# Input projection of a hybrid trunk step: 26 of 28 pairs of weight tiles by seven half-size block products in place of eight

## What is computed

```
h = rms_norm(x, g_norm) * (1 + scale) + shift          # scale, shift, gate from silu(c) @ w_ada
proj = h @ w_in                                         # 1024 -> 7168
u   = proj[glu_value] * sigmoid(proj[glu_gate])
y   = silu(layer_norm(depthwise_conv31(u)))
y_a = (y * silu(proj[conv_z])) @ w_a_out
p   = windowed_mean(proj[pool_in]) - proj[pool_in]      # windows 2, 4, 8, 16 by group
y_b = (group_matmul(p) * scale * silu(proj[pool_z])) @ w_b_out
m   = sigmoid(proj[merge_a]) * y_a + sigmoid(proj[merge_b]) * y_b
out = rms_norm(x + gate * (m @ w_out), g_final)         # and the new states of both branches
```

## Time and profile before

| | us |
|---|---|
| median of 3 runs | 993.92 (993.38 to 994.63) |
| profiled execution, its own time | 993.59 |
| span of the profiled execution | 991.8 |
| TensorE busy in the span | 977.4 |
| VectorE busy | 664.6 |
| ScalarE busy | 245.4 |
| mean granted clock of TensorE | 0.997 of full speed |

### The profile page before, as it was taken

How to read it: one execution, slowest core, us unless ns; L and a number is a source line. 1 busy time by engine, 2 the same in 40 slices (tenths; PEclk the granted TensorE clock), 3 DMA queues, 4 the chain that set the end, 5 groups by cost and what they waited for, 6 DMA issues and landing times.

```text
span 991.8 us, 14051 instructions
## 1 busy us (share of the span) xinstructions
PE 977.4 (99%) x6256; PEld 960.1 (97%) x6256; DVE 664.6 (67%) x666; ACT 245.4 (25%) x263; POOL 1.9 (0%) x12
## 2 busy tenths in 40 slices
PE   8999999999999999999999999999999999999997
PEld 5699999999999999999999999999999998999996
DVE  1868985727897663888764689969878743342346
ACT  5331122221212221112212111123623512122242
POOL 0000000000000000000000000000000000000000
PEclk9999999999999999999999999999999999999998
DMA  9612221231230231122024122113961173124104
GB/s 373 251 44 64 88 78 55 86 122 43 67 116 27 97 123 48 59 86 97 28 76 142 43 76 100 55 54 129 368 250 43 36 306 128 43 88 190 43 1 171
DMA packets 32252, 106.46 MB, mean 107 GB/s; under 512 B 7616, under 2 KB 14144, under 8 KB 28736
## 3 DMA queue, kind: packets, MB, share of 16 engines
q1 hardware_dynamic: 28016, 92.75, 26.7%
q10 hardware_dynamic: 4176, 12.82, 3.4%
HBM read 82.76 MB, written 22.79 MB: 106 GB/s over the span
## 4 chain that ended last, share of the span: by engine, by line
PE 96%; DMA 1%; DVE 1%; ACT 0%; issue 0%; SPq 0%; DVEq 0%
PE ps L490 31%; PE ps L493 31%; PE ps L491 31%; DMA bf<-x_t 1%; PE aux L420 1%; DVE bf L948 1%; PE aux L426 0%; PE aux L472 0%; DVE hf L1202 0%; PE ps L420 0%; PE aux L663 0%; PE ps L433 0%; PE aux L655 0%; PE ps L467 0%; ACT L755 0%
## 5 line engine op out<-in xcount | busy, mean ns | idle before, releaser
L491 PE MATMUL ps<-hr,w_hi 128*128 128x344 f32 x1536 | 486.8, 320 | 0.0
L490 PE MATMUL ps<-hr,w_hi 128*128 128x344 f32 x1344 | 426.5, 320 | 0.6 <-DVE hr L957 0.6
L981 DVE SCALAR_TENSOR_TENSOR conv_y<-conv_u,par_all,conv_y 128x1024 f32<-128x1024 f32 x240 | 308.1, 1284 | 22.6 <-PE ps L493 16.0
L491 PEld LDWEIGHTS ps<-hr,w_hi 128*128 128x128 f32 x1536 | 289.2, 188 | 0.0
L493 PE MATMUL ps<-hr,w_lo 128*128 128x344 f32 x1344 | 285.1, 320 | 0.0
L490 PEld LDWEIGHTS ps<-hr,w_hi 128*128 128x128 f32 x1344 | 253.1, 188 | 2.4 <-issue 1.6
L493 PEld LDWEIGHTS ps<-hr,w_lo 128*128 128x128 f32 x1344 | 224.9, 188 | 0.0
L906 DVE TENSOR_TENSOR w_lo<-w_raw,w_hi 128x1024 fp32r<-128x1024 f32 (+1 forms) x86 | 98.8, 1149 | 83.7 <-ACT w_hi L706 80.8
L706 ACT ACTIVATE w_hi<-w_raw 128x1024 fp32r<-128x1024 f32 (+1 forms) x86 | 85.5, 995 | 280.2 <-PE ps L493 269.4
L490 PE MATMUL ps<-gr,w_hi 128*128 128x344 f32 x384 | 123.3, 324 | 0.0
L491 PE MATMUL ps<-gr,w_hi 128*128 128x344 f32 x384 | 121.8, 320 | 0.0
(11 more groups left out here) (129 smaller groups left out, 564.8 us busy)
## 6 DMA issues: line engine op xcount, KB each, us to landing
w_raw<-w_main SPq DMA_DIRECT2D x78, 512.0 KB, 3.6
ada_raw<-w_ada SPq DMA_DIRECT2D x8, 1024.0 KB, 20.2
bf<-x_t SPq DMA_DIRECT2D x4, 1032.0 KB, 8.6
sig_a<-stage_lo ACTq DMA_DIRECT2D x8, 516.0 KB, 2.6
sig_b<-stage_hi ACTq DMA_DIRECT2D x8, 516.0 KB, 2.7
y_conv<-conv_y SPq DMA_DIRECT2D x8, 516.0 KB, 3.0
silu_z<-stage_hi ACTq DMA_DIRECT2D x8, 516.0 KB, 3.6
bf<-y_conv SPq DMA_DIRECT2D x4, 1032.0 KB, 7.1
```

What stands on the lines that cost most here:

```text
L490: nc.tensor.matmul(out, wh, rhs_hi[:, cols(c)], start=(k == 0), stop=False)
L491: nc.tensor.matmul(out, wh, rhs_lo[:, cols(c)], start=False, stop=False)
L981: return v.scalar_tensor_tensor(out=y, in0=conv_u[:, x, k:k + SEQ], scalar=par_all[:, g, x, k:k + 1], in1=y, op0=ALU.mult, op1=ALU.add)
```

## The change

A pair is now the two tiles of one part of the projection (output channels 0 to 127 and 128 to 255 of it). With the weights cut into input-channel halves and the activation into input-channel halves and token halves (516 columns), a pair is a 2 x 2 by 2 x 2 block product. In the form with seven products, P1 to P7, four of them use sums of weight blocks and four use sums of activation blocks. A product ("item") is 4 steps over input channels, each with 6 matmuls of 258 columns, 24 in all.

What is new, by engine:

- **TensorE**: 4 jobs as before (`FIRST_JOBS`, two pairs of merge tiles), then 190 items: 26 pairs x 7 and 8 `MIX` items of 24 matmuls. Products of one pair and of the next alternate (`item_table`). P1, P6, P7 and P4 accumulate in one bank pair, P2 in another, P5 and P3 in a third.
- **ScalarE**: 190 splits of half a weight tile (512 columns), for each pair three copies of 516 columns of intermediate sums (`seeded`, `u2`, `u3`), and the sigmoid or silu of four half rows in two steps. Before the items it rewrites the 8 tiles of `h` in full (`h_full_done`) and splits the four activation sums (`tr`, 2,064 columns each).
- **VectorE**: 190 half-size lo splits (`item_lo_part`), two additions of 516 columns for each pair (`results`), and for `glu_value` also the products with the gate. Before the items it makes the four activation sums `t1` to `t4` and their lo parts. Taps of the two tiles of a group alternate, and a tap waits for the last tap of its own tile only. Their place is now computed by `tap_table` from a table of costs: after each item ("slot") taps are added until the budget of the slot is used up. At the slot where the next `glu_value` pair reaches P5 all taps left are put (`due`).
- **GpSimd**: makes the four weight sums of each pair from DRAM to DRAM, in 13 rounds of 8 DMAs (4 plain copies, 4 with addition) of 512 KB. A round serves two pairs and is a chain of six steps, each waiting for the one before; it begins when the modulation weights have been loaded.
- **SyncE**: loads half weight tiles (256 KB) four items ahead, P3, P5, P6 and P7 from `w_sums`. The results of the first six tiles of the pooling branch go to DRAM (`b`) and come back before the `w_b_out` jobs.

The jobs for `w_b_out` begin with their first four steps for two jobs together, then wait for `y_summed`. All later jobs are unchanged. The arithmetic of all outputs is the same sum, in another order.

The core of the diff:

```diff
-PAIR_JOBS = [
-    ("glu_gate", 0, "act"), ("glu_value", 0, "dve"), ("glu_gate", 1, "act"), ("glu_value", 1, "dve"),
-    ("merge_a", 0, "act"), ("merge_a", 1, "act"), ("merge_b", 0, "act"), ("merge_b", 1, "act"),
-    ("pool_in", 0, "act"), ("pool_in", 1, "act"), ("pool_z", 0, "act"), ("pool_z", 1, "act"),
-    ("pool_mix", 0, "dve"), ("conv_z", 0, "act"), ("pool_mix", 1, "dve"), ("conv_z", 1, "act"),
-]
...
+FIRST_JOBS = [("merge_a", 0), ("merge_a", 1), ("merge_b", 0), ("merge_b", 1)]
...
+PAIR_ORDER = [
+    ("glu_gate", 0), ("glu_value", 0), ("pool_in", 0), ("pool_z", 0), ("merge_a", 1), ("conv_z", 0),
+    ("glu_gate", 1), ("glu_value", 1), ("pool_in", 1), ("pool_z", 1), ("merge_b", 1), ("conv_z", 1),
+    ("glu_gate", 2), ("glu_value", 2), ("pool_in", 2), ("pool_z", 2), ("merge_a", 2), ("conv_z", 2),
+    ("glu_gate", 3), ("glu_value", 3), ("pool_in", 3), ("pool_z", 3), ("merge_b", 2), ("conv_z", 3),
+    ("merge_a", 3), ("merge_b", 3),
+]
...
+MIX_IN = {5: (0, 0), 6: (0, 1), 11: (1, 0), 12: (1, 1), 17: (2, 0), 18: (2, 1), 23: (3, 0), 24: (3, 1)}
...
-TAPS_AT = {1: (1, 4), 2: (2, 5), 3: (0, 5), 4: (2, 5), 5: (2, 5), 6: (2, 5), 7: (2, 5), 8: (0, 1), 9: (0, 1), 10: (0, 4),
-           12: (0, 6), 14: (0, 5)}
...
+def item_table():
+    items = []
+    for n in range(N):
+        items.append(("P1", n))
+        if n:
+            items.append(("P3", n - 1))
+        items.append(("P6", n))
+        if n:
+            items.append(("P4", n - 1))
+        items.append(("P7", n))
+        if n in MIX_IN:
+            items += [("MIX", n), ("P2", n), ("P5", n)]
+        else:
+            items += [("P5", n), ("P2", n)]
+    return items + [("P4", N - 1), ("P3", N - 1)]
...
+SUM_OF = {"P5": 0, "P6": 1, "P7": 2, "P3": 3}
...
+T_OF = {"P6": 0, "P7": 1, "P5": 2, "P4": 3}
...
+SLOT_COST = 2745
+LAG = 1500
+COST = {"lo": 580, "half": 680, "tap": 1165, "first_tap": 1900, "last_tap": 2270, "level": 1130, "out": 2100, "pool_lo": 1150, "mix": 1370}
...
+        due = g + 1 < PAIRS and slot == AT["P5", PAIR_OF["glu_value", g + 1]]
+        while left[0] + left[1]:
+            x = 1 - last_x if left[1 - last_x] else last_x
+            cost = COST["first_tap" if left[x] == CONV_W else "last_tap" if left[x] == 1 else "tap"]
+            if not due and clock + cost > late + (slot + 1) * SLOT_COST + LAG:
+                break
+            taps[slot].append((g, x))
+            left[x] -= 1
+            clock += cost
+            last_x = x
+        if due:
+            late = max(late, clock - (slot + 1) * SLOT_COST - LAG)
...
+            pool.wait_ge(ada_loaded[3][1], 16)
+            for c in range(N // 2):
+                if c >= 4:
+                    pool.wait_ge(item_done, AT["P1", 2 * c - 8] + 1)
+                first = FIRST_PAIR_BLOCK + 4 * c
+                tiles0, tiles1 = (t["w_main"][first + x:first + 4:2].rearrange("a p c -> p a c") for x in range(2))
+                a11, a12 = tiles0[:, :, 0:FORM_COLS], tiles0[:, :, FORM_COLS:]
+                a21, a22 = tiles1[:, :, 0:FORM_COLS], tiles1[:, :, FORM_COLS:]
+                s1, s2, s3, s4 = (t["w_sums"][2 * c:2 * c + 2, k].rearrange("a p c -> p a c") for k in range(4))
+                pool.dma_start(s1, a21).then_inc(sum_copied, 16)
+                pool.dma_start(s3, a21).then_inc(sum_copied, 16)
+                pool.wait_ge(sum_copied, 64 * c + 32)
+                pool.dma_start(s1, a22, accum_op=ALU.add).then_inc(sum_added, 16)
+                pool.dma_start(s3, a11, accum_op=ALU.add).then_inc(sum_added, 16)
+                pool.wait_ge(sum_added, 64 * c + 32)
+                pool.dma_start(s2, s1).then_inc(sum_copied, 16)
+                pool.wait_ge(sum_copied, 64 * c + 48)
+                pool.dma_start(s2, a11, accum_op=ALU.add).then_inc(sum_added, 16)
+                pool.wait_ge(sum_added, 64 * c + 48)
+                pool.dma_start(s4, s2).then_inc(sum_copied, 16)
+                pool.wait_ge(sum_copied, 64 * c + 64)
+                pool.dma_start(s4, a12, accum_op=ALU.add).then_inc(sum_added, 16)
+                pool.wait_ge(sum_added, 64 * c + 64)
...
-            def pair_job(g, i):
-                kind, tile, _ = PAIR_JOBS[i]
-                pe.wait_ge(w_lo_done, 2 + g * JOBS_PER_PAIR + (i + 1))
...
+            def block_product(q, bank, x_hi, x_lo, n_k=KH, start=False):
+                wh, wl = ring(q)
+                for k in range(n_k):
+                    w_cols = slice(k * P, (k + 1) * P)
+                    for c in range(2):
+                        t_cols = slice(c * QW, (c + 1) * QW)
+                        nc.tensor.matmul(bank[:, c, :], wh[:, w_cols], x_hi[:, k, t_cols], start=start and k == 0, stop=False,
+                                         skip_group_check=True)
+                        nc.tensor.matmul(bank[:, c, :], wh[:, w_cols], x_lo[:, k, t_cols], start=False, stop=False,
+                                         skip_group_check=True)
+                    for c in range(2):
+                        t_cols = slice(c * QW, (c + 1) * QW)
+                        last = nc.tensor.matmul(bank[:, c, :], wl[:, w_cols], x_hi[:, k, t_cols], start=False, stop=(k == n_k - 1),
+                                                skip_group_check=True)
+                return last
...
+                if form == "P1":
+                    if n == 0:
+                        pe.wait_ge(act_evac, 3)
+                    elif n == 1:
+                        pe.wait_ge(act_evac, 4)
+                    else:
+                        pe.wait_ge(c21_out, n - 1)
+                    if n - 1 in MIX_IN:
+                        pe.wait_ge(mix_out, sum(m < n for m in MIX_IN))
+                    block_product(q, bank_a(n), hr[:, 0:KH, HALVES[0]], hr[:, KT:KT + KH, HALVES[0]], start=True).then_inc(item_done, 1)
+                if form == "P6":
+                    pe.wait_ge(seeded, n + 1)
+                    t_product(q, bank_a(n), form)
+                if form == "P7":
+                    pe.wait_ge(u2_ready, n + 1)
+                    t_product(q, bank_a(n), form)
+                if form == "P4":
+                    pe.wait_ge(u3_ready, n + 1)
+                    t_product(q, bank_a(n), form)
+                if form == "P2":
+                    pe.wait_ge(seeded, n + 1)
+                    block_product(q, bank_b, hr[:, KH:KT, HALVES[0]], hr[:, KT + KH:2 * KT, HALVES[0]]).then_inc(item_done, 1)
+                if form == "P5":
+                    if n:
+                        pe.wait_ge(c12_out, n)
+                    if n in MIX_IN:
+                        pe.wait_ge(mix_out, sum(m <= n for m in MIX_IN))
+                    t_product(q, bank_c, form, start=True)
+                if form == "P3":
+                    pe.wait_ge(c22_out, n + 1)
+                    block_product(q, bank_c, hr[:, KH:KT, HALVES[1]], hr[:, KT + KH:2 * KT, HALVES[1]]).then_inc(item_done, 1)
...
+            def item_lo_part(q):
+                n = item_columns(q)
+                dve.wait_ge(item_hi, q + 1)
+                hi, lo = ring(q)
+                v.tensor_tensor(lo[:, 0:n], raw4[:, q % 4, 0:n], hi[:, 0:n].bitcast(F32), ALU.subtract).then_inc(item_lo, 1)
...
+                if form == "P5":
+                    dve.wait_ge(item_done, slot)
+                    dve.wait_ge(u3_ready, n + 1)
+                    row_free(n, 1)
+                    row = row_of(n, 1)[:, second]
+                    v.scalar_tensor_tensor(out=halves(row), in0=bank_c, scalar=-1.0, in1=halves(u3[:]), op0=ALU.mult, op1=ALU.subtract).then_inc(c22_out, 1)
+                    if kind in ("glu_value", "pool_in"):
+                        dve.wait_ge(c22_out, n + 1)
+                    if kind == "glu_value":
+                        dve.wait_ge(act_out, ACT_OUT["C22", n - 1])
+                        link(v.tensor_tensor(row, row, sig[:, 1, second], ALU.mult))
+                    if kind in ("glu_value", "pool_in"):
+                        state_column(n, 1)
...
+            for slot in range(LAST + 1):
+                if slot:
+                    results(slot)
+                item_lo_part(slot + 2)
+                if slot in POOL_STEPS:
+                    pool_step(*POOL_STEPS[slot])
+                if slot in POOL_LO_AT:
+                    pool_lo(*POOL_LO_AT[slot])
+                for g, x in TAPS[slot]:
+                    tap(g, x)
```

863 lines of the change are left out of this document (575 added, 288 removed).

## The result

The changed kernel takes **983.86 us** (median of 8 runs, 982.04 to 989.75), the kernel before 994.14 (993.38 to 994.63, 8 runs beside them): a ratio of 0.9905, 95% interval 0.9892 to 0.9918. It is faster, by 10.3 us where the prediction had 34. It lies inside the upper end of the range (984) by 0.1 us, which is luck: the forecast's own case (950 to 968) does not reach it, and no bound stood for what went wrong. The profiled execution took 982.33 us for a span of 980.4.

A forecast was written before the change was run, and what follows sets the result against it. TensorE was taken to bound the kernel before, VectorE every round of the changed one. Span 991.8 - 613.4 + 562 (items) + 7 (start) + 11 (end) = 958.4 us, plus 1.8 outside it: 960 us; range 937 to 984.

The forecast's parts named there:

- the forecast's own case: Whole kernel: VectorE sets the rounds' pace, 960 us, spanning 950 to 968 with its bounds at start and end; chance 0.45.
- The stretch of the items: Jobs 4 to 63, now the items: 14 slots 38.4, four rounds 514.5, three times 3, together 562 us against 613.4.
- three times 3: Behind each stop at a round's end: VectorE runs dry for about 3 us, counted three times.
- The matmul at 114 ns: TensorE's items: a 258-column matmul takes 114 ns, between 107.5 + 14.4 = 121.9 and the weight load's 111.
- VectorE's prices and its pace: Rounds of items: taps 1.21 us, splits 0.60, half results 0.67, levels 1.25; VectorE sets the pace of every round.
- The stops: Ends of rounds, where 6, 8 and 9 taps stand before P5: TensorE waits some 6, 8 and 10 us.
- Rival 2: In the stops: the granted clock falls, slow items behind waits cost 5 to 15 us, total 968; chance 0.20.
- The start, +7: Before the items: rewrites of h delay job 2 by 5 us, waits of P6 and P7 add 2; range 3 to 12.
- The end, +11: Behind the last item: TensorE waits 5 us until y_summed, then 6 or 7 at the sums of squares; range 4 to 18.
- At nothing: In the items: ScalarE's work and the weight loads cost no time, loads having 8 us of cover against 3.6.
- Rival 1: VectorE cheaper than read, alternating taps at 1.14 us: stretch 548 us, at most down to 540, total 938 to 946; chance 0.22.
- Rival 3: GpSimd's weight sums come late: a round takes 30 us, as slow as before from 46; chance 0.13, 0.10 for slower than before.

The follow-up runs named there:

- e9: Changed kernel with item products run over 242 of each 258 columns, so a matmul takes 114 ns: 980.63 us, ratio 0.9871 to the kernel before.
- e5: Changed kernel with 42, 62 and 80 idle products put where TensorE stops before P3 of glu_value: 979.03 us, ratio 0.9845; the first output is off.
- e1: No part of the layer: 96 matmuls of each kind alone, at several widths, in fp32r and bf16; the program took 337 us (one run).
- e3: Changed kernel with only SLOT_COST raised from 2745 to 2920 in the table that deals out the taps: 979.04 us, ratio 0.9854 to the kernel before.
- e11: e10 plus the other row's taps due a slot later, SLOT_COST 2920 without lag before mix results, and tail operations moved: 974.34 us, ratio 0.9801.
- e2: Changed kernel with taps 1 to 29 of both tiles left out in the first three rounds (174 taps): 967.44 us, ratio 0.9724 to the kernel before.
- e7: Changed kernel with job 0's evacuation and job 2's weight splits moved between the fourth and fifth rewrite of h: 986.14 us, ratio 0.9915.
- e8: e2 with GpSimd's sums in four chained steps in place of six, 11 DMAs in place of 8: 1045.19 us, ratio 1.0516 to the kernel before.
- e10: e7 with GpSimd's sums overlapped, four steps per two pairs in place of six, same 8 DMAs and bytes: 984.71 us, ratio 0.9907.
- e4: Changed kernel with GpSimd's weight sums left out, summed tiles loaded from the plain weights: 982.25 us, ratio 0.9882 to the kernel before.
- e12: e11 with each load of a summed tile waiting for its own sum in place of all four: 970.49 us, ratio 0.9763 to the kernel before.

## Why the prediction was wrong, point by point

**The stretch of the items: the step that failed.** The prediction added 14 slots, four rounds of 41, 41, 41 and 45 slots and "three times 3" us of VectorE run dry. These are 182 of 190 items. The windows of 41 slots are those in which taps may be applied; the three items behind each stop were left out of the sum but for 3 us. Those 3 us were VectorE's idle time there, and its own work in these slots was charged nowhere. With 2.74 us an item the three are 8.2 us each, and the first round's window opens at item 13 where I counted 14. Mended: 562 + 3 x 5.2 - 2.7 = 575 us. e9, with just the price I had assumed, measured 573.1, and its last three rounds are 136.2, 138.7 and 129.3 us where the mended sum has 136.5, 139.0 and 129.6. The measured stretch is 578.4, so 16.4 us were missed. The slip is worth up to 13 of them. The matmul's price gave 5.3 (e9) and the clock 4.6 (e5), each measured with the other left in; if the two simply add, 6.5 are left for the slip. No run has both, so its share between 6.5 and 13 us stays open.

**The matmul at 114 ns.** It is 120.5 in the kernel and 120.7 alone (e1). The rows had a lower bound (the load, 111) and an upper one (the surcharge, 121.9), and I took a value near the lower for no better reason than that stream and load are alike. It was worth only 5.3 us (e9) of the 30, since VectorE hid the rest. "Nearly independent of whether a matmul takes 111 or 118 ns" held.

**VectorE's prices and its pace.** Right. Taps came 1.20 us apart (forecast 1.21), splits 0.60, half results 0.61 to 0.67 (0.67), levels 1.25. "VectorE sets the pace of every round" held for three of four (e9); the fourth was TensorE's. The margin is small: without taps the first round is 127.1 us, with them 132.2, so that taps cost just their stop. Neither engine's work was cut alone with much gain.

**The stops.** 5.24, 7.63 and 9.70 us where 6, 8 and 10 were forecast, before the third item behind each piece, released by VectorE's lo split, as said.

**Rival 2, the clock.** It happened together with the forecast's case, while I had it as another case. The granted clock was 0.5 behind every stop, at 64.4 to 71.2 us in the wait for job 2 and at 685.6 and 702.7 in the tail. It costs 4.6 us in the items (e5). A matmul of 344 columns starts 0.287 us behind the last one there and 0.158 at full clock. The 19 of them at the start lost 2.4 us by that, the 31 in the tail 4.2. Together 11 us, of which e5 shows the first part by experiment. The rule of the Trainium skill ("TensorE: Matmul & The Clock Gate", on loop structure) that I had set against my sum was right. Its 968 us was my sum with the same slip in it.

**The start, +7.** 8.0 measured. Job 2 began at 65.95 us (forecast 65.6, +5.4), and the fall of the clock added 2.4. The waits of P6 and P7 of pair 0 (1.1 and 1.0 us, forecast 2) lie within the items.

```profile
52.94 8.42 ACT L1090 ACTIVATE bf<-bf,mod 128x1024 f32<-128x1024 f32 x8
61.37 1.28 ACT L1094 ACT_TABLE_LOAD   x1
...
65.95 0.66 PE L762 MATMUL ps<-hr,w_hi 128*128 128x344 f32 x1 [4.81 <-DVE w_lo L1295]
```

These answer to the earlier trace rows: eight rewrites, the table, the evacuation, then the lo part that job 2 waits for.

**The end, +11.** 15.5 measured, and at other places than forecast: 1.4 us at the first job behind the items and 2.5 at `y_summed` (forecast 5 together), then 6.8 not at the variance sums but a job earlier. VectorE has the lo part of the third merge_b job's weights behind six centred tiles and one evacuation, and these wait for DMAs:

```profile
694.33 7.30 DVE L1573 TENSOR_TENSOR bf<-bf,row_mean 128x1032 f32<-128x1032 f32 x6 [4.36 <-DMA bf<-y_conv]
704.32 1.23 DVE L1568 TENSOR_TENSOR hf<-ps,hf 128x1032 f32<-128x1032 f32 x1 [2.69 <-DMA hf<-sig_b]
705.47 1.22 DVE L1295 TENSOR_TENSOR w_lo<-w_raw,w_hi 128x1024 fp32r<-128x1024 f32 x1
```

The sum of the waits, 10.7 us, is what I had forecast; the clock (4.2) is what I had not. Much of it can be had back: e3, with no tap left over for the tail, took 5.0 us less there, and e11, which also moved those operations, 7.8.

**At nothing.** It held in the items of the changed kernel: P6 and P7 aside, no wait for ScalarE or for a load.

**Rival 1** fell: the taps were as dear as read. **Rival 3** did not happen, but was nearer than the 0.13 says: I took 30 us for a round of sums with a break-even of 46; it took 43 on average ((596.1 - 38.4)/13), from 38 to 52. e2, e7 and e8 turned it into the bound with small edits, and e10 brought it down to 35. An "at nothing" for the sums in the changed kernel is right (e4) and says nothing of how much it has to spare.

**The sum.** 958.4 + 16.4 for the stretch + 1.0 for the start + 4.5 for the rest = 980.3, the measured span to 0.1. That must come out, since the span was cut in these three parts; what stands behind each part is said above.

## What to carry to other kernels

When a forecast adds up rounds, count the items in it against the items of the program: this one missed eight of 190, and with them 6.5 to 13 of the 16 us that its main term was off. Where two engines are both busy over 90% of a stretch, expect little from cutting one: here 30 us off TensorE gave 5, and 208 us off VectorE 9, with another 14 lost to waits that came up behind the sums. Price the half-speed work behind a wait of TensorE along with the wait, and don't take many short waits for cheaper than a few long ones: e3's sixteen waits cost 7.3 us that way, the changed kernel's three stops 5.1. Before moving a start forward ask what else must then be early: here the sums, and the condition on which their loads wait (e12).

## What the runs showed of the hardware

- An fp32r matmul costs 13 to 16 ns over its columns at 258 and 344 columns (e1), and 120.9 ns at 258 even where its weights stay the same; a bf16 one of 258 columns costs 2.5 over them.
- The granted clock can fall without a pause. In the program of e1 TensorE was busy throughout with matmuls of 64 and then 128 columns, which at the lower clock start 213 ns apart at either width, and these rows (the columns as above) show the clock fall in the first kind, stay low in the second and rise in the third, 192 columns wide; 258 columns ran at 1.00:

```profile
139.60:156.80 17.20, 17.20 (x97) 17.20 (x96) 0.00 (x0) 0.00 (x0) 0.00 (x0) 0.60 0.00 0
156.80:177.30 20.50, 20.50 (x97) 20.50 (x98) 0.00 (x0) 0.00 (x0) 0.00 (x0) 0.50 0.00 1
177.30:191.20 13.90, 13.90 (x98) 13.90 (x98) 0.00 (x0) 0.00 (x0) 0.00 (x0) 0.76 0.01 1
202.80:214.60 11.80, 11.80 (x99) 11.80 (x98) 0.00 (x0) 0.00 (x0) 0.00 (x0) 1.00 0.00 0
```

- DMAs from DRAM to DRAM in pieces of 512 KB, in the changed kernel: a copy with no other sum beside it lands after 4.2 us, such an addition after 6.2 to 6.9, and of two additions issued together the first after 6.0 and the second after 9.7 (medians of 13). More of them in flight make each longer, but not the whole: two pairs' 8 DMAs took 42.9 us in the changed kernel and 34.7 chained closer (e10), 4.3 us each. The 11 of e8 took 49.3, 4.5 each.
- Short waits bring the lower clock too. In e3 the granted clock is 0.5 for 3.4 us with or just behind each of five waits of 2.3 to 3.5 us.
